# A routed-expert stage on one Trainium2 core: blocks taken from both halves of the sorted list, weights gathered by row number

## What is computed

```
idx  = top 8 of 64 experts for each of T = 1024 tokens (from the 4 best of 8 groups)
sizes  = bincount(idx, 64);  padded = ceil(sizes / 128) * 128
block_e = for each block of 128 sorted rows: its expert, min(searchsorted(cumsum(padded), 128*b, right), 63)
y[b] = (silu(xb @ w_gate[e]) * (xb @ w_up[e])) @ w_down[e]      # xb (128, 1024), gate/up (1024, 256), down (256, 1024)
out[token] += gate_weight * its row of y ;  out += shared expert(h) ;  x = x + g2 * out ;  rmsnorm
```

## Time and profile before

| what | value |
|---|---|
| runs, median of 3 (lowest to highest) | 4628.94 us (4622.33 to 4638.01) |
| the profiled execution, its own time | 4627.36 us |
| its span, first to last instruction | 4625.1 us |
| mean granted TensorE clock | 0.928 of 2.4 GHz |
| busy: PE, DVE, ACT, POOL | 4062.8, 1684.2, 1205.4, 719.3 us |
| moved by DMA | 795.16 MB, mean 172 GB/s |
| `experts`, first gate/up matmul to the last down product | about 3376 to 4473 us |

### The profile page before, as it was taken

How to read it: one execution, slowest core, us unless ns; L and a number is a source line. 1 busy time by engine, 2 the same in 40 slices (tenths; PEclk the granted TensorE clock), 3 DMA queues, 4 the chain that set the end, 5 groups by cost and what they waited for, 6 DMA issues and landing times. The chain is left out here.

```text
span 4625.1 us, 74505 instructions
## 1 busy us (share of the span) xinstructions
PE 4062.8 (88%) x29460; PEld 2648.0 (57%) x29460; DVE 1684.2 (36%) x2437; ACT 1205.4 (26%) x1715; POOL 719.3 (16%) x554
## 2 busy tenths in 40 slices
PE   6999888887979998888879978887889999999963
PEld 3888667665547887666655544535544444444423
DVE  3355554553341004545533426522511111111128
ACT  1111354442221112454422334412111111111114
POOL 2222122120122221131111100000010000000014
PEclk8999998898999999998889989997999999999985
DMA  6765333113313423331123217001089999999967
GB/s 218 216 220 177 124 112 123 53 44 117 127 68 134 141 100 121 107 126 63 39 88 123 86 44 295 35 32 58 19 303 356 351 360 359 356 357 355 355 249 263
DMA packets 289081, 795.16 MB, mean 172 GB/s; under 512 B 29377, under 2 KB 121026, under 8 KB 252994
## 3 DMA queue, kind: packets, MB, share of 16 engines
q1 hardware_dynamic: 240738, 616.41, 38.3%
q10 hardware_dynamic: 25632, 93.33, 5.0%
q0 software_dynamic: 22464, 81.80, 4.9%
HBM read 622.64 MB, written 160.43 MB: 169 GB/s over the span
## 5 line engine op out<-in xcount | busy, mean ns | idle before, releaser
L463 PE MATMUL ps<-s_proj_hS,s_proj_wS 128*128 128x512 f32 x3216 | 768.7, 402 | 62.5 <-POOL s_proj_wS L353 62.5
L463 PEld LDWEIGHTS ps<-s_proj_hS,s_proj_wS 128*128 128x128 f32 x3216 | 615.0, 192 | 212.3 <-ACT s_proj_wS L413 63.4
L518 PE MATMUL ps<-gate_h,gate_w 128*128 128x512 f32 x1536 | 417.9, 424 | 33.8 <-PEq L146 19.3
L518 PEld LDWEIGHTS ps<-gate_h,gate_w 128*128 128x128 f32 x1536 | 296.2, 198 | 136.9 <-issue 52.1
L3181 PE MATMUL ps<-s_exp_gu,keep_hT 128*128 128x512 f32 x736 | 340.9, 606 | 19.8 <-DMA s_exp_gu<-in_w_gu_dram 18.0
L3165 PE MATMUL ps<-s_exp_wd,s_exp_aT 128*128 128x512 f32 x736 | 331.2, 593 | 1.9 <-ACT s_exp_aT L3091 1.9
L3186 PE MATMUL ps<-s_exp_gu,keep_hT 128*128 128x512 f32 x736 | 330.8, 592 | 0.0
L505 POOL TENSOR_TENSOR gate_w<-gate_raw,gate_w 128x512 fp32r<-128x512 f32 x128 | 186.4, 1459 | 824.3 <-ACT gate_w L499 823.5
L3131 DVE TENSOR_TENSOR s_exp_sg<-s_exp_sg,ps 128x256 f32<-128x256 f32 x92 | 38.7, 421 | 666.6 <-ACT s_exp_sg L3112 666.6
L353 POOL TENSOR_TENSOR s_proj_wS<-s_proj_w,s_proj_wS 128x1024 fp32r<-128x1024 f32 x67 | 174.0, 2599 | 565.4 <-ACT s_proj_wS L413 565.4
L381 DVE COPY s_proj_o<-ps 128x512 f32<-128x512 f32 x66 | 45.5, 690 | 570.3 <-PE ps L463 570.3
(11 more groups left out here) (451 smaller groups left out, 5854.1 us busy)
## 6 DMA issues: line engine op xcount, KB each, us to landing
s_exp_gu<-in_w_gu_dram SPq DMA_DIRECT2D x184, 1024.0 KB, 10.8
s_exp_wd<-in_w_down_dram SPq DMA_DIRECT2D x92, 1024.0 KB, 9.1
yrow<-keep_hT ACTq DMA_DIRECT2D x92, 512.0 KB, 9.5
keep_mix<-in_w_ada_dram SPq DMA_DIRECT2D x80, 512.0 KB, 6.0
s_proj_w<-in_w_in_dram SPq DMA_DIRECT2D x66, 512.0 KB, 4.6
proj<-s_proj_o ACTq DMA_DIRECT2D x66, 512.0 KB, 2.7
gate_raw<-in_w_in_dram SPq DMA_DIRECT2D x128, 256.0 KB, 3.1
yrow<-keep_xT SPq DMA_DIRECT2D x4, 8192.0 KB, 49.1
```

The costliest lines, as they stand in the source:

```text
L463: mm = pe.matmul(k.ps[:, 6 + half if last else 2 * b + half, :], wS[:, b, x, t, :], hS[:, y, t, half * HALF:(half + 1) * HALF], start=(t = ...
L518: mm = pe.matmul(self.k.ps[:, self.banks[g // 2], :], weight[:, w, t - t0, :], self.k.hG[:, h, t, :], start=(t == 0 and w + h == 0), stop= ...
```

## The change

Four things change.

1. The order of blocks. `sorted_place` maps round i, buffer u to a place in the sorted list: buffer 0 walks places 0, 1, 2, ... and buffer 1 walks the second half, from the number of rounds on. So blocks of one expert follow each other in the same buffer. y goes to the same sorted place, and `combine` is as it was.
2. The weight loads leave SyncE, which has nothing left to do in `experts`, and become three indirect DMAs on GpSimd (L3082 of the changed kernel), each of 128 rows of 8 KB. Their row numbers are in `k.wrow`, made in `route`: 128 e + p for the down weights and twice that for gate/up. The rows of a block whose expert is that of the place before it, and that does not begin a half, get 2^20 added (doubled for gate/up), which is beyond `bounds_check`, and nothing is loaded: the buffer keeps what it has.
3. GpSimd's order: the x gather of a block comes between the second gate/up load and the down load of the block before it.
4. In `route` VectorE makes `k.wrow` instead of `ebi` (a diagonal matrix, one matmul with ones on TensorE, ten small operations), and SyncE's store and reload of the expert numbers go.

Of the 92 blocks, with 64 experts and the sizes above, 64 are the first of their expert in their buffer, and 28 are repeats (one of them the padding block).

```diff
@@ Kernel.second_block
-        self.eb = self.keep("eb", [1, P], I32)
+        self.wrow = self.keep("wrow", [P, NBLK, 2], I32)
@@ used_rounds
+FAR = 1 << 20
...
-    yield 0, False
-    yield 1, False
+    yield 0, final, False
+    yield 1, final, False
...
-            yield i, False
-    yield final, True
+            yield i, final, False
+    yield final, final, True
@@ route, sync
-            sp.wait_ge(eb_ready, 1)
-            sp.dma_start(ebd[:, :], ebi[:]).then_inc(st_eb, 16)
-            sp.wait_ge(st_eb, 16)
-            sp.dma_start(k.eb[:], ebd.rearrange("p o -> o p")).then_inc(ld_back, 16)
-            sp.wait_ge(ld_back, 16)
@@ route, vector
+            mine.do(dve.tensor_scalar(hi[:], end[:, NE - 1:NE], 1.0, None, ALU.add))
+            mine.do(dve.tensor_scalar(hi[:], hi[:], 1, None, ALU.arith_shift_right))
+            mine.do(dve.tensor_copy(hf[:], hi[:]))
...
-            dve.tensor_copy(ebi[:], ebf[:]).then_inc(eb_ready, 1)
+            dve.tensor_scalar(ebdiag[:], k.eye[:], ebf[:, 0:1], None, ALU.mult).then_inc(eb_ready, 1)
             shared(1)
+            dve.wait_ge(ebrow_ready, 1)
+            mine.do(dve.tensor_copy(ebrow[:], k.ps[:, 7, 0:NBLK]))
+            mine.mark(dve.tensor_scalar(fresh[:], iota[:], hf[:, 0:1], None, ALU.is_equal))
+            mine.settle()
+            tt(ebdiag[:, 1:NBLK], ebrow[:, 1:NBLK], ebrow[:, 0:NBLK - 1], ALU.not_equal)
+            tt(fresh[:, 1:NBLK], fresh[:, 1:NBLK], ebdiag[:, 1:NBLK], ALU.max)
+            mine.do(dve.memset(fresh[:, 0:1], 1.0))
+            mine.do(dve.tensor_scalar(fresh[:], fresh[:], -1.0, -float(FAR), ALU.add, ALU.mult))
+            mine.do(dve.tensor_scalar(ebrow[:], ebrow[:], float(P), pidx[:, 0:1], ALU.mult, ALU.add))
+            tt(ebrow[:], ebrow[:], fresh[:], ALU.add)
+            mine.mark(dve.tensor_copy(k.wrow[:, :, 1], ebrow[:]))
+            mine.mark(dve.tensor_scalar(k.wrow[:, :, 0], ebrow[:], 2.0, None, ALU.mult))
+            mine.settle()
@@ route, tensor
+            pe.wait_ge(eb_ready, 1)
+            pe.matmul(k.ps[:, 7, 0:NBLK], k.ones[:], ebdiag[:], start=True, stop=True).then_inc(ebrow_ready, 1)
             pe.wait_ge(act_ready, 2)
@@ experts, sync (the whole block goes)
-                    e = sp.value_load(k.eb[0:1, b:b + 1] if isinstance(b, int) else k.eb[0:1, bass.ds(b, 1)],
-                                      min_val=0, max_val=NE - 1)
...
@@ experts, gpsimd
+        def sorted_place(i, final, u):
+
+            return final + (i + 1) if u else i
...
+            def rows(i, final, u):
+                b = i * 2 + u
+                wait(pool, ld_x[u], i * 16, 16)
+                wait(pool, xtr_ready, b - 1)
+                pool.tensor_copy(idx[:, u:u + 1], k.idx[:, bass.ds(sorted_place(i, final, u), 1)]).then_inc(idx_ready, 1)
...
+            def part(u, dst, table, offset, signal):
+                src, c = (I["w_gu"].rearrange("e p (h t) n -> (e p h) (t n)", h=2), 0) if table == "gu" else \
+                    (I["w_down"].rearrange("e p f n -> (e p) (f n)"), 1)
+                pool.indirect_dma_start(dst, None, src, bass.IndirectOffsetOnAxis(ap=wrow[:, u, c:c + 1], axis=0), element_offset=offset,
+                                        bounds_check=(2 - c) * NE * P - 1, oob_is_err=False).then_inc(signal, 16)
+
+            for i, final, last in used_rounds(pool, k):
+                if isinstance(i, int) and i == 0:
+                    rows(0, final, 0)
                 for u in range(2):
                     b = i * 2 + u
+                    wait(pool, ld_wd[u], i * 16, 16)
+                    wait(pool, gu_half, b - 1)
+                    pool.tensor_copy(wrow[:, u:u + 1, :], k.wrow[:, bass.ds(sorted_place(i, final, u), 1), :]).then_inc(wrow_ready, 1)
+                    pool.reg_mov(wcopied, wfollowing)
+                    pool.wait_ge(wrow_ready, wcopied)
+                    pool.reg_add(wfollowing, wcopied, 1)
+                    part(u, gu[:, u, 0:KH].rearrange("p t n -> p (t n)"), "gu", 0, ld_ga[u])
+                    wait(pool, gu_ready, b - 1)
+                    part(u, gu[:, u, KH:KT].rearrange("p t n -> p (t n)"), "gu", 2 * D, ld_gb[u])
+                    if not (last and u):
+                        rows(i + 1 if u else i, final, 1 - u)
+                    wait(pool, down_ready, b - 1)
+                    part(u, wd[:, u].rearrange("p f n -> p (f n)"), "down", 0, ld_wd[u])
@@ experts, scalar (store)
-                act.dma_start(yrow[:, bass.ds(b, 1), :], y[:, u:u + 1, :]).then_inc(st_y[u], 16)
+                act.dma_start(yrow[:, bass.ds(sorted_place(i, final, u), 1), :], y[:, u:u + 1, :]).then_inc(st_y[u], 16)
```

More of the change, by code:

```diff
@@ L2798, in route @@
         sg = hrow[:, 0]
-        names = ("ld_wr ld_c ld_s ld_d lg_ready sc_ready own mask_ready rank_ready hot_ready hot_done eb_ready st_eb ld_back "
+        names = ("ld_wr ld_c ld_s ld_d lg_ready sc_ready own mask_ready rank_ready hot_ready hot_done eb_ready ebrow_ready "
                  "h_ready h_taken st_h0 st_h1 g_ready u_ready sg_ready act_ready d_ready d_taken tq")
-        (ld_wr, ld_c, ld_s, ld_d, lg_ready, sc_ready, own, mask_ready, rank_ready, hot_ready, hot_done, eb_ready, st_eb,
-         ld_back, h_ready, h_taken, st_h0, st_h1, g_ready, u_ready, sg_ready, act_ready, d_ready, d_taken, tq) = (
+        (ld_wr, ld_c, ld_s, ld_d, lg_ready, sc_ready, own, mask_ready, rank_ready, hot_ready, hot_done, eb_ready, ebrow_ready,
+         h_ready, h_taken, st_h0, st_h1, g_ready, u_ready, sg_ready, act_ready, d_ready, d_taken, tq) = (
             s.sem(n) for n in names.split())
@@ L2805, in route @@
         block = s.block()
-        ebd = k.scratch["ebd"]
         @block.sync
@@ L3038, in experts @@
         hrow = k.scratch["hrow"]
-        @block.sync
-        def _(sp):
-            for i, last in used_rounds(sp, k):
-                for u in range(2):
-                    b = i * 2 + u
-                    e = sp.value_load(k.eb[0:1, b:b + 1] if isinstance(b, int) else k.eb[0:1, bass.ds(b, 1)],
-                                      min_val=0, max_val=NE - 1)
-                    wait(sp, gu_half, b - 1)
-                    sp.dma_start(gu[:, u, 0:KH], I["w_gu"][e, :, 0:KH]).then_inc(ld_ga[u], 16)
-                    if isinstance(b, int) and b == 0:
-                        sp.wait_ge(ld_x[0], 16)
-                    wait(sp, gu_ready, b - 1)
-                    sp.dma_start(gu[:, u, KH:KT], I["w_gu"][e, :, KH:KT]).then_inc(ld_gb[u], 16)
-                    wait(sp, down_ready, b - 1)
-                    sp.dma_start(wd[:, u], I["w_down"][e]).then_inc(ld_wd[u], 16)
+        def sorted_place(i, final, u):
+            return final + (i + 1) if u else i
         @block.gpsimd
@@ L3058, in _ @@
             copied, following = pool.alloc_register("copied"), pool.alloc_register("following")
+            wcopied, wfollowing = pool.alloc_register("wcopied"), pool.alloc_register("wfollowing")
             pool.reg_mov(following, 1)
-            for i, last in used_rounds(pool, k):
+            pool.reg_mov(wfollowing, 1)
+            def rows(i, final, u):
[3 more added lines that the diff above has]
+                pool.tensor_copy(idx[:, u:u + 1], k.idx[:, bass.ds(sorted_place(i, final, u), 1)]).then_inc(idx_ready, 1)
+                pool.reg_mov(copied, following)
+                pool.wait_ge(idx_ready, copied)
+                pool.reg_add(following, copied, 1)
+                pool.indirect_dma_start(x[:, u, :], None, hrow, bass.IndirectOffsetOnAxis(ap=idx[:, u:u + 1], axis=0))\
+                    .then_inc(ld_x[u], 16)
@@ L3101, in store @@
                 wait(act, y_dve, b + 1)
-                act.dma_start(yrow[:, bass.ds(b, 1), :], y[:, u:u + 1, :]).then_inc(st_y[u], 16)
+                act.dma_start(yrow[:, bass.ds(sorted_place(i, final, u), 1), :], y[:, u:u + 1, :]).then_inc(st_y[u], 16)
             turned(act, 0, 0, 0, put, xt_act)
-            for i, last in used_rounds(act, k):
+            for i, final, last in used_rounds(act, k):
                 for u in range(2):
@@ L3115, in _ @@
                     if not (isinstance(b, int) and b == 0):
-                        store(i if u else i - 1, b - 1, 1 - u)
+                        store(i if u else i - 1, final, b - 1, 1 - u)
             turn_a(b)
-            store(i, b, 1)
+            store(i, final, b, 1)
         @block.vector
@@ L3125, in _ @@
             turned(dve, 0, 0, 1, put, xt_dve)
-            for i, last in used_rounds(dve, k):
+            for i, final, last in used_rounds(dve, k):
                 for u in range(2):
@@ L3169, in _ @@
             turn_x(0, 0, 0)
-            for i, last in used_rounds(pe, k):
+            for i, final, last in used_rounds(pe, k):
                 for u in range(2):
```

23 lines of the change are left out of this document (9 added, 14 removed).

## The result

| | before | after |
|---|---|---|
| median of 5 runs each (lowest to highest) | 4629.64 us (4622.33 to 4638.01) | 4601.97 us (4592.97 to 4603.20) |
| ratio, 95% interval | 1 | 0.9937 [0.9921, 0.9953] |
| profiled execution, span, granted clock | 4627.36, 4625.1 us, 0.928 | 4601.97, 4600.2 us, 0.925 |
| `experts`, start of the first gate/up product to that of the last | 3376.22 to 4457.14: 1080.9 us | 3383.03 to 4435.87: 1052.8 us |

The medians lie 27.7 us apart; by the ratio the changed kernel is 0.63% faster. The last line of the table is the best measure of the stage, since it holds nothing of the spread of what runs ahead of it; it fell by 28.1 us.

A forecast was written before the change was run, and what follows sets the result against it. Transfers were taken to bound `experts`, 11.78 us a block against TensorE's 11.48. Terms -25 + 1 - 1 + 0.1 = -25 us from 4627.36 gave 4602, or 4604 as that execution lay 1.6 below the median; range 4593 to 4639.

The forecast's parts named there:

- the transfers set the pace: Middle of `experts`: transfers need 11.78 us a block at 356 GB/s, TensorE 11.48, so transfers bound by 0.285 us.
- Traffic removed: In `experts`, 28 of 92 blocks load no weights, 88 MB less; TensorE becomes the bound at 11.48: 25 us saved at most.
- Residual waits: Blocks in `experts` that load everything, third or later in their run, may still wait: +1 us, ends 0 and 7.5.
- GpSimd's issues at 1.0 us: Each weight load in `experts` holds GpSimd 1.0 us; it is busy 7.0 us a block, under 11.48: cost 0.
- The margin of 1.3 us: In `experts`, the first gate/up load lands at 3810.8 and is wanted at 3812.09, where the queue was clear.
- One queue for weights and x: Moving the weights of `experts` to queue q0 with x keeps 356 GB/s, and the later x gather is not late: 0.
- Start: Start of `experts`: x goes first and lands 2.1 us earlier, weights go out 2.8 us later: -1 us, between -2 and +3.
- Skipped rounds: Seventeen unused rounds before the last of `experts`: GpSimd issues the last loads no later than SyncE did: 0, up to +3.
- route: VectorE's additions in `route` mostly fit within 10 us of slack; about 0.1 us falls ahead of the shared down product: +0.1 us.
- A: Rival: weight loads above 2.48 us make GpSimd the bound in `experts`; 4663 us at 2.7, 4742 at 3; chance 0.14.
- B: Rival: queue q0 is slower with weights, 25 blocks wait; 4638 us at 327 GB/s, 4624 at 341; chance 0.12.
- C: Rival: rows out of bounds cost their transfer all the same, nothing is saved; 4627 to 4631 us; chance 0.08.

The follow-up runs named there:

- e1: The changed kernel with a repeat's rows kept in bounds, so all 92 blocks load their weights: 4612.84 us, ratio to before 0.9969.
- e7: The kernel before with the down load put behind the next block's two gate/up loads, on SyncE: 4598.98 us, ratio to before 0.9950.
- e2: The changed kernel with only each half's first block loading weights, 2 of 92: 4596.76 us, ratio to before 0.9927.
- e9: The kernel before with x row numbers out of bounds from block 4 on, so those gathers move nothing: 4601.45 us, ratio to before 0.9954.
- e10: The changed kernel with a GpSimd memset of 3.51 us a block ahead of the first gate/up load: 4640.78 us, ratio to before 1.0031.
- e6: As e1, but the x gather goes ahead of the first gate/up load on GpSimd: 4654.59 us, ratio to before 1.0063.
- e4: The kernel before with the second gate/up load bringing three of its four tiles from round 2 on: 4627.26 us, ratio to before 0.9997.
- e5: The kernel before with the x gather held back until the first gate/up load of block b-2 has landed: 4656.16 us, ratio to before 1.0068.
- e11: The kernel before with the second gate/up load bringing two of its four tiles from round 2 on: 4621.93 us, ratio to before 0.9991.
- e8: The changed kernel with the down load behind the two gate/up loads and one more row-number copy: 4593.32 us, ratio to before 0.9939.
- e12: As e8, but in round 0 the first gate/up load goes ahead of the first x gather: 4601.00 us, ratio to before 0.9937.

## Why the prediction was right, and where its reasons were not

4604 us was predicted and 4602 measured, and the middle of the stage reads as forecast: 11.4 us a block, 282 GB/s, L3082 at 1.0 us. But the size was right for a reason that the runs bear out only in part, and that the sum met the time was partly luck: the step that claimed 25 us for the bytes gave 8.0 us by the stage time, and steps priced at nothing gave the rest, 20.1 us in the stage and 3.4 us behind it.

- **What bounds: "the transfers set the pace".** This step failed. The working divided the bytes of a block by the rate of the same stretch, and so had to find the block's own period, whatever bounded it: 356 GB/s was a result of the pace. The same bytes went at 362 (e1) and 366 GB/s (e7). What set the pace was the time between A's request and its use, with Down in front of it and x beside it. The 10.0 us of lead and the 10.9 us of landing (a median over A and B together) stood in the text, and were the better reading. The 24.3 us of waits, taken as a second proof, added the wait of the matmuls (17.8) to that of TensorE's weight loads (6.5), which overlap them; against the period of 11.40 the same 85 blocks lost 31 us.
- **Traffic removed, -25.** The most that could be saved was the waits, and that was rightly taken as the limit, but its floor was 0.08 us too high. Between the two products of the earlier trace rows that I took as free of waits lay a small one; the true floor is 11.40 (e2, e7, e9), and 88 x 0.365 = 32 us could be had, which is what e9 had. The bytes gave only 8.0 of the 28.1 us (e1 to after).
- **Residual waits, +1, with 7.5 as end.** 4.2 us by stage time (after against e2), inside the ends.
- **GpSimd's issues at 1.0 us, cost 0.** Right: 0.987 to 1.037 us for each of the 276, a chain of 6.3 us a block from Down to the end of x's gather where 7.0 was worked out. The margin of 1.3 us was too small: e10 took 2.96 us from it and paid 0.67, so it is 2.0 to 2.7 us, by what the block before loads.
- **One queue for weights and x, 0.** The rate held: q0 alone moved 317 MB in e1. By the 341 GB/s of the Trainium skill ("DMA: Bandwidth & Descriptors", measured rates for loads issued from GpSimd) e1 would have had a period of 12.3 us, an estimate, with waits in every block; the trace doesn't agree, with a mean of 11.54 us. But the step gave x's place behind two weight loads no price, and that place is the likely source of e1's 20.1 us: e9 shows that the waits of before go with x beside A, and e6 that in one queue x ahead of A, with A's later request, costs more than all of them. A shorter lead goes against it, and yet e1 waited less: A's lead is 8.6 us in e1 for 10.3 before (medians). Whether the one queue in place of two has a share of its own in the 20.1 wasn't taken apart.
- **Start, -1, between -2 and +3.** +0.5. x did come sooner, but the first load, sent off last, was waited for 3.1 us.
- **Skipped rounds, `route`.** 0 and +0.1 as worked out, measured -0.1 and +0.1.
- **Left out.** From the start of the last gate/up product to `combine`'s first gather it is 25.8 us for 29.2. In the profiles where SyncE issues the weights (before, e4, e5, e7, e9, e11) it is 29.2 to 29.9; where GpSimd issues them (the other eight) 25.8 to 28.2. GpSimd's drain in the barrier accounts for the step between the two: 7.574 us in each of the first six, 4.144 in each of the eight. The rest of the spread lies ahead of it. Why that drain is shorter stays open. The prediction had said that it would be wrong if `route` or `combine` moved by over 3 us; `combine`, from its first gather to the end, took 138.5 us for 138.7, so it was the barrier, which the prediction had not priced.

Of the rivals, A fell with L3082 at 1 us. B fell with e1: had q0 been slower with weights, all blocks loading would have been worse than before. C fell with the 282 MB, but so did its price. With nothing skipped I gave it 4627 to 4631 us, and e1, which is that case made, took 4613.

## What to carry to other kernels

A rate worked out from a stretch in which the consumer sets the pace is no ceiling; before cutting bytes, set for the latest load the time from its request to its use beside the time it takes to land, and look at what is asked for in front of it and runs beside it. A load whose request stands behind a wait for another buffer can often be asked for a block earlier at no cost, and here that alone gave what the whole change gave. A queue's order is a lever too: what is needed last goes last, and moving the non-urgent gather a few us "out of the way" can put it in the way of the next block.

## What the runs showed of the hardware

- An indirect load all of whose rows are out of bounds holds GpSimd as long as a real one: gate/up has a median of 1006 ns in e2, where 90 of 92 blocks are out of bounds, and of 1002 in e1, where none is; the x gather takes 1018 ns in e9 for 966 before, with the bounds check added. It still makes small packets, and in e9 an x gather of nothing took 3.2 us (median) from issue to landing, for 6.2 with its 0.5 MB.
- DMA engines 0.96 to 0.97 busy did not mean that the rate was at its limit: at that share the kernel before moved 356 GB/s, e1 362 and e7 366.
- GpSimd's drain in the barrier behind `experts` took 7.574 us in every profile in which GpSimd had gathered x alone, and 4.144 us in every profile in which it had issued the weights too.
- Most of the spread between profiles lies ahead of the experts. In the 14 profiles GpSimd's first copy of the stage came between 3360.7 and 3373.0 us, with the same instructions ahead but for the small differences in `route`, while the five kernels without waits (e2, e7, e8, e9, e12) agree in stage time within 1.5 us. `combine`, from its first gather on, took 138.1 to 141.3 us. Hence stage times are the sharper measure for the stage, though each is from one profile, and e4 and e11 show in them what the runs can't tell.
